# One run per partition for the experts' down weights, and stepped columns of the gate and up weights

## The reference

```python
def one_block(args):
    tok_b, w_b, e = args
    xb = x_pad[tok_b]
    hb = jax.nn.silu(xb @ w_gate[e]) * (xb @ w_up[e])
    return (hb @ w_down[e]) * w_b[:, None]
```

## Time and profile before

| | |
|---|---|
| Profiled execution | 1739.24 us |
| Its span, first to last instruction | 1737.5 us |
| TensorE matmul busy | 1604.0 us, 92% |
| TensorE weight load busy | 1159.7 us, 67% |
| VectorE busy | 1123.2 us, 65% |
| ScalarE busy | 897.7 us, 52% |
| GpSimd busy | 608.5 us, 35% |
| Moved by DMA | 457.45 MB in 156011 packets |
| Granted TensorE clock, mean | 0.964 of full speed |

### The profile page before, as it was taken

The page is one execution under the profiler, slowest core; times in us unless marked ns, Lnnn a source line. Parts: engine busy times, 40 slices in busy tenths (PEclk is TensorE's granted clock), DMA queues, the critical chain, the costliest instruction groups (busy, mean ns, idle before and its releaser), DMA issues.

```text
span 1737.5 us, 26456 instructions
## 1 busy us (share of the span) xinstructions
PE 1604.0 (92%) x8785; PEld 1159.7 (67%) x8786; DVE 1123.2 (65%) x1575; ACT 897.7 (52%) x1389; POOL 608.5 (35%) x555
## 2 busy tenths in 40 slices
PE   5999999689989898777999999999999999999997
PEld 4555545333436666635888888888888888888843
DVE  3255576552234546477877888788788788778746
ACT  1011101142335555415777777777777777777733
POOL 0056677400000000013344454554555555555310
PEclk9999999879999899977999999999999999999999
DMA  9688867577774211574999999999999999999884
GB/s 339 214 279 294 274 219 225 166 258 247 218 233 140 79 55 44 208 294 176 332 302 313 322 315 326 314 325 338 324 327 337 335 320 335 333 315 337 281 260 178
DMA packets 156011, 457.45 MB, mean 263 GB/s; under 512 B 25375, under 2 KB 35806, under 8 KB 138458
## 3 DMA queue, kind: packets, MB, share of 16 engines
q1 hardware_dynamic: 119289, 368.12, 58.8%
q0 software_dynamic: 26624, 69.80, 15.9%
q10 hardware_dynamic: 9960, 17.83, 3.0%
HBM read 394.52 MB, written 78.15 MB: 272 GB/s over the span
## 4 chain that ended last, share of the span: by engine, by line
PE 37%; DMA 7%; DVE 6%; ACT 3%; issue 3%; POOL 1%; POOLq 0%; ACTq 0%; DVEq 0%
PE ps L2428 10%; PE ps L2388 7%; PE ps L2407 7%; DMA acc_d<-yb,tokb 7%; PE ps L2366 3%; PE ps L2390 3%; PE ps L2764 2%; DVE lo_dn L2463 2%; PE ps L2782 1%; PE ps L2393 1%; DVE lo_gu L2463 1%; DVE xT_h L2470 1%; ACT hi_dn L2275 1%; ACT xT_h L2282 1%; PE ps L1872 1%
## 5 line engine op out<-in xcount | busy, mean ns | idle before, releaser
L2463 DVE TENSOR_TENSOR lo_gu<-raw_gu,hi_gu 128x1024 fp32r<-128x1024 f32 x252 | 297.4, 1221 | 53.5 <-ACT hi_gu L2275 53.0
L2388 PE MATMUL ps<-xT_h,hi_gu 128*128 128x416 f32 (+4 forms) x896 | 269.9, 364 | 3.3 <-DVE xT_h L2470 1.9
L2220 POOL DMA_INDIRECT acc_d<-yb,tokb x96 | 162.5, 1693 | 253.6 <-ACT yb L2328 241.4
L2275 ACT ACTIVATE hi_gu<-raw_gu 128x1024 fp32r<-128x1024 f32 x252 | 251.3, 1048 | 0.0
L602 PE MATMUL ps<-w_in_sb,hT 128*128 128x512 f32 x512 | 225.2, 598 | 1.1 <-ACT hT L466 1.1
L2390 PE MATMUL ps<-xT_h,lo_gu 128*128 128x208 f32 (+4 forms) x896 | 225.2, 251 | 0.0
L446 POOL TENSOR_TENSOR prod<-kring,qbc 128x512 f32<-128x512 f32 x128 | 159.3, 1272 | 175.0 <-DMA kring<-in_cache_k 120.2
L2197 POOL DMA_INDIRECT xg<-h_d,tokb x96 | 139.9, 1458 | 159.0 <-PE ps L2366 116.9
L602 PEld LDWEIGHTS ps<-w_in_sb,hT 128*128 128x128 f32 x512 | 96.5, 191 | 118.5 <-issue 117.1
L2428 PE MATMUL ps<-hi_dn,hT_h 128*128 128x512 f32 (+5 forms) x512 | 170.9, 400 | 5.1 <-DVE hb_l L2503 4.9
L2388 PEld LDWEIGHTS ps<-xT_h,hi_gu 128*128 128x128 f32 x896 | 169.5, 189 | 7.6 <-issue 2.6
(11 more groups left out here) (364 smaller groups left out, 3011.4 us busy)
## 6 DMA issues: line engine op xcount, KB each, us to landing
raw_gu<-in_expert_w_gate SPq DMA_DIRECT2D x64, 1024.0 KB, 10.3
raw_gu<-in_expert_w_up SPq DMA_DIRECT2D x64, 1024.0 KB, 15.0
raw_dn<-in_expert_w_down SPq DMA_DIRECT2D x64, 1024.0 KB, 11.0
kring<-in_cache_k SPq DMA_DIRECT2D x128, 256.0 KB, 3.1
vring<-in_cache_v SPq DMA_DIRECT2D x128, 256.0 KB, 3.0
adaw<-in_ada_w ACTq DMA_DIRECT2D x7, 2048.0 KB, 13.3
adaw<-in_ada_w SPq DMA_DIRECT2D x5, 2048.0 KB, 15.4
w_in_sb<-in_w_in SPq DMA_DIRECT2D x4, 2048.0 KB, 19.9
```

Source lines behind the costliest of these rows:

```text
L2220: pool.indirect_dma_start(out=acc_d[b % 2][:, :], out_offset=bass.IndirectOffsetOnAxis(ap=tokb[0:rows, b:b + 1], axis=0), in_=yb[b % 2][0: ...
L2275: act.activation(hi_cut(n, u), raw_cut(n, u), ACT.Copy).then_inc(hi_made, 1)
L2388: pe.matmul(ps[:, bank, 0:2 * cap], wh, x[:, k, :, :].rearrange("p a t -> p (a t)"), start=(k == 0), stop=False)
L2463: dve.tensor_tensor(lo_cut(n, u), raw_cut(n, u), hi_cut(n, u).bitcast(F32), ALU.subtract).then_inc(lo_made, 1)
```

## The change

`load_down` reads the down weights as `(p c)` instead of `(c p)`: partition p gets rows 2p and 2p+1, which lie together in memory, as one run of 8 KB. Partition j of half ch is now hidden unit 2j + ch. To match, the heavy expert's stationary operand takes every second column of the 256 (128 floats, 8 bytes apart) instead of 128 neighbouring ones, for gate and up, hi and lo. `turn_h` transposes every second column of the light expert's hidden rows instead of 128 neighbouring ones. Everything else is as before.

```diff
         def load_down(sp, n, e):
-            w_from, = addressed(sp, ew_down[0][bass.ds(e, 1)].rearrange("o (c p) n -> p (o c) n", p=P))
-            sp.dma_start(raw_dn[n % RAWS][:, :, :], w_from).then_inc(dn_in[n % RAWS], 16)
+            w_from, = addressed(sp, ew_down[0][bass.ds(e, 1)].rearrange("o (p c) n -> p (o c n)", c=FC))
+            sp.dma_start(raw_dn[n % RAWS].rearrange("p c n -> p (c n)"), w_from).then_inc(dn_in[n % RAWS], 16)
...
                     for k in range(KC):
                         if h == 0 and ch == 0 and k % 2 == 0:
                             pe.wait_ge(lo_made, nth_cut[n, k // 2])
-                        cols = slice(k * F + ch * P, k * F + (ch + 1) * P)
-                        wh, wl = hi_gu[n % 2][:, h, cols], lo_gu[n % RAWS][:, h, cols]
+                        wh, wl = (w[:, h, k * F:(k + 1) * F].rearrange("p (j c) -> p c j", c=FC)[:, ch, :]
+                                  for w in (hi_gu[n % 2], lo_gu[n % RAWS]))
...
                 for ch in range(FC):
-                    last = pe.transpose(ps[:, gate_bank(p), ch * P:(ch + 1) * P], hb_l[:, ch * P:(ch + 1) * P], ident)
+                    last = pe.transpose(ps[:, gate_bank(p), ch * P:(ch + 1) * P], hb_l.rearrange("t (p c) -> t c p", c=FC)[:, ch, :], ident)
                 last.then_inc(h_tr, 1)
```

## The result

The changed kernel takes 1747.28 us (median of 19 runs, 1742.64 to 1751.51), the kernel before 1740.15 us in the runs beside it (19 runs, 1733.35 to 1745.1). The ratio is 1.0037, with a 95% interval of 1.0027 to 1.0046: about 6.4 us slower, well under the 1% that was called no change, but clear of zero. The forecast was 1748, and 4.3 us of cost.

A forecast was written before the change was run, and what follows sets the result against it. TensorE was taken to bound the expert stage, pacing the transfers. 1739.24 + 0 + 4.1 + 0.2 = 1743.5 us on the profiled execution, 1748 with the 4.2 us by which the median stands above it; range 1720 to 1795.

The forecast's parts named there:

- What bounds: Expert stage: TensorE busy 695.09 of 700 us is the bound; the DMA share of 0.97 is paced by TensorE.
- Part 1: Down loads in 8 KB runs: 45 us of landing time gained, none reaching the end; term 0.
- cover of 34.7 us: Time from a heavy expert's down load issue to ScalarE's first read, against a longest landing of 17.1 us.
- Part 2: Heavy gate/up products: stepped loads behind short matmuls are exposed, 1024 loads at 4 ns each, +4.1 us.
- the longer of two limits, not their sum: Stepped heavy load takes the longer of its two limits, 4 ns more; if the surcharge adds up, 56 ns.
- Part 3: Transposes of the light hidden rows, 64 stepped, loads from 139 to about 195 ns; +0.2 us.
- The step adding up: Rival, heavy gate/up products: 56 ns more on each of 1024 exposed loads, together +66 us, 1809; chance 0.17.
- Rows gathered late: Rival, token-row gathers sharing the 16 engines: 0.2 us late, two a pair, 13 us, 1761; chance 0.08.
- The DMA engines in the way: Rival: easier loads remove ScalarE's 17.6 us wait for the scatter-add, which delays TensorE; faster, 1726; chance 0.08.

The follow-up runs named there:

- the run alone: Down weights in one 8 KB run per partition, gate/up columns and transpose left contiguous, against the kernel before: 1740.90 us against 1738.45, ratio 1.0016.
- hi +5.2: Only the heavy expert's hi loads stepped, lo loads and all else as in the kernel before: 1742.77 us, ratio 1.0030.
- lo none: Only the heavy expert's lo loads stepped, all else as in the kernel before: 1738.13 us, ratio 0.9998.
- wide matmuls: Every lo matmul over 2*cap columns, in the kernel before and in the changed one: 1798.50 and 1799.70 us, ratios to the kernel before 1.0316 and 1.0327.
- issued late: Kernel before with down loads issued most of a pair later, in 4 KB runs 1752.63 us, in 8 KB runs (contiguous columns) 1749.79 us.

## Why the prediction was right

**What bounds.** Right. The DMA share of 0.97 was a paced queue: the landing of the down loads fell by a quarter, and with the run alone nothing was gained.

**The number.** The forecast of 1748 is 0.7 us from the measured 1747.28, and a closeness of that kind is in part luck. The base of 1743.46 us was the median of three runs, and stands 3.3 us above the 1740.15 of nineteen; the cost of 4.3 us was 2.1 too low. The two errors go opposite ways.

**Part 1, the run: term 0.** Right as to a gain. I had the landing from 11.0 to near 10.3; it went to 8.3, and it still did not matter, since the cover of 34.7 us was no nearer to being used up, and even with 12 us left no engine waited for a down load. The +2.5 us of the run alone is a small miss that the runs don't explain.

**Part 2, the step: +4.1 us.** The mechanism was right: the load behind the short matmul is the exposed one (hi +5.2, lo none, with wide matmuls +1.2; by the pairs 7 ns, 1 and 1). The size was off. The term took 4 ns a load from the dense stream of stepped transposes; the loads rose by 7 (188 to 195), and the pairs by 8.75 in the mean, 9.0 us in all, of which about 6 reach the end. The row I set aside, the step of two in the finish stage (195 ns), had the value of the load exactly. And I chose the reading (the longer of two limits, not their sum) for the cadence of the transposes. The choice was right at a step of two and its reason was not: at a step of four the transposes went on at 0.95 us for eight and the matmuls' loads more than doubled their hold on the path, to 235 ns. Had the change had a step of four, the same argument would have missed by some 175 us. The Trainium skill, page SBUF — State Buffer, section Door 1, asks for two hits to a 16-byte line, and says that four fp32 is the step still free. For the loads of fp32r matmuls the runs agree with the first in the main (7 ns at a step of two, 141 at four) and disagree with the second.

**Part 3, the light transpose: +0.2.** The load went to 198 ns (195 expected), and two transposes take 0.23 us in the chain instead of 0.22. Too small to be told in the time.

**The rivals.** The step adding up (loads of 244 ns) didn't come: 195. Rows gathered late: TensorE never waits for xg in the steady stage, though the longest landing went from 12.9 to 14.6 us, past the 13.5 us of cover read from one gather; the median, 10.3 before, is 10.1. The DMA engines in the way: ScalarE's wait for the scatter is 20.4 us, not less than 17.6.

## What to carry to other kernels

Ask which engine paces a busy DMA queue before making its transfers cheaper: here a landing shorter by a quarter was worth nothing. Find the short matmuls whose next weight load doesn't fit behind them; here each ns on those loads cost about a ns, on the others almost nothing. A layout that suits the DMA is paid for by whoever reads it in steps, so price that reader by a record of the same kind of instruction, not of a neighbouring one.

## What the runs showed of the hardware

- A fp32r weight load of 128 columns holds its path for about 107 ns when contiguous, some 7 ns more at a step of 8 bytes, and 235 ns at 16 bytes (records 188, 195, 329 ns; 338 at 32 bytes). The loads of transposes record 139, 195 to 198, 211 and 192 ns at steps of 4, 8, 16 and 32 bytes.
- ScalarE writing 128x1024 to fp32r with neighbouring elements 1 KB apart took about 2.0 us instead of 1.04; VectorE reading one operand so lost a few per cent at most (1246 against 1221 ns in the mean).
- A 1 MB load in one run of 8 KB per partition lands in a median of 8.1 and 8.3 us in two kernels, where two runs of 4 KB took 10.0 and 11.0, in the same stage and place (7.8 and 9.8 when issued late).
